# Five of 192 expert weight slabs loaded by two transfers of 8 partitions and one of 112

## The reference

```python
def ec_moe(u, w_router, w_gate, w_up, w_down):
    ...
    aff = jax.nn.softmax((u @ w_router).astype(jnp.float32), axis=-1)
    gates, idx = lax.top_k(jnp.swapaxes(aff, 1, 2), cap)
    xs = u[bidx, idx]
    hid = jax.nn.silu(jnp.einsum('becd,edf->becf', xs, w_gate)) * jnp.einsum('becd,edf->becf', xs, w_up)
    ys = jnp.einsum('becf,efd->becd', hid, w_down) * gates[..., None].astype(u.dtype)
    return jnp.zeros_like(u).at[bidx, idx].add(ys)
```

## Time and profile before

| what | value |
|---|---|
| median of three runs | 2798.47 us |
| profiled execution, its own time | 2803.4 us |
| its span in the trace | 2801.6 us |
| TensorE matmul busy | 2374.1 us, 85% |
| VectorE busy | 1193.8 us, 43% |
| mean rate of the transfers | 247 GB/s |

### The profile page before, as it was taken

One profiled execution on the slowest core, in us unless ns is written; L12 is line 12 of the kernel. 1 busy time (PEld: TensorE's weight loads), 2 busy tenths in 40 slices (PEclk: granted clock), 3 DMA queues, 4 the chain that ended last, 5 costly groups with the idle time before them and its releaser, 6 DMA issues.

```text
span 2801.6 us, 45258 instructions
## 1 busy us (share of the span) xinstructions
PE 2374.1 (85%) x19841; PEld 1843.7 (66%) x19841; DVE 1193.8 (43%) x2238; ACT 512.2 (18%) x1145; POOL 189.6 (7%) x322
## 2 busy tenths in 40 slices
PE   7999988555655665556899999999999999999999
PEld 4667774111211121111699988999999998899999
DVE  2555632000000000000566667774665666776555
ACT  4434421000000000000210125411011012451200
POOL 0363610000000000000000001000000000100000
PEclk9999989888887777877999999999999999999999
DMA  7534439999999999999644354344454444434443
GB/s 259 157 101 133 139 116 417 428 428 427 427 428 427 427 428 426 425 428 427 267 166 174 128 174 163 133 171 160 167 178 153 171 175 160 146 133 167 165 154 118
DMA packets 212625, 691.38 MB, mean 247 GB/s; under 512 B 36876, under 2 KB 76237, under 8 KB 186829
## 3 DMA queue, kind: packets, MB, share of 16 engines
q1 hardware_dynamic: 204685, 683.74, 63.3%
q10 hardware_dynamic: 7744, 4.75, 0.6%
HBM read 684.23 MB, written 4.23 MB: 246 GB/s over the span
## 4 chain that ended last, share of the span: by engine, by line
PE 62%; DMA 30%; DVE 4%; ACT 2%; issue 1%; SPq 0%; POOL 0%; ACTq 0%; DVEq 0%
PE bank L1958 18%; PE bank L2008 10%; DMA slab_ring_more<-in_moe_w_up 7%; PE bank L2210 6%; DMA slab_ring<-in_moe_w_up 6%; DMA slab_ring_more<-in_moe_w_gate 6%; PE bank L401 5%; DMA slab_ring_more<-in_moe_w_down 5%; DMA slab_ring<-in_moe_w_down 5%; PE bank L2303 4%; PE bank L1425 3%; PE bank L2051 3%; PE bank L1925 2%; PE bank L2106 1%; PE bank L2186 1%
## 5 line engine op out<-in xcount | busy, mean ns | idle before, releaser
L1425 PE MATMUL bank<-slab_ring,chosen_xT 128*32 128x512 f32 x1248 | 199.5, 775 | 123.3 <-DMA slab_ring<-in_moe_w_up 66.6
L1958 PE MATMUL bank<-slab_ring 128*128 128x128 f32 x2560 | 299.1, 275 | 1.8 <-ACT lru_gelu L2419 1.8
L1958 PEld LDWEIGHTS bank<-slab_ring 128*128 128x128 f32 x2560 | 292.3, 192 | 2.2 <-issue 2.2
L1587 DVE TENSOR_TENSOR beaten_then_hidden<-bank,beaten_then_hidden 128x512 f32<-128x512 f32 x16 | 11.1, 691 | 562.6 <-PE bank L1425 562.6
L1958 PE MATMUL bank<-layer_uT,slab_ring 128*128 128x128 f32 x1920 | 227.5, 275 | 0.0
L1958 PEld LDWEIGHTS bank<-layer_uT,slab_ring 128*128 128x128 f32 x1920 | 221.1, 192 | 0.2
L1425 PEld LDWEIGHTS bank<-slab_ring,chosen_xT 128*32 128x32 f32 x1248 | 38.9, 127 | 276.2 <-DMA slab_ring<-in_moe_w_up 110.7
L1425 PE MATMUL bank<-slab_ring_more,chosen_xT 128*32 128x512 f32 x800 | 135.4, 812 | 99.9 <-DMA slab_ring_more<-in_moe_w_up 56.8
L2008 PE MATMUL bank<-slab_ring 128*128 128x128 f32 x1408 | 165.7, 275 | 0.0
L2008 PEld LDWEIGHTS bank<-slab_ring 128*128 128x128 f32 x1408 | 161.4, 192 | 0.0
L1425 PEld LDWEIGHTS bank<-slab_ring_more,chosen_xT 128*32 128x32 f32 x800 | 25.2, 129 | 200.8 <-DMA slab_ring_more<-in_moe_w_up 87.3
(11 more groups left out here) (482 smaller groups left out, 3691.8 us busy)
## 6 DMA issues: line engine op xcount, KB each, us to landing
slab_ring<-in_w_up SPq DMA_DIRECT2D x44, 2048.0 KB, 8.0
slab_ring<-in_moe_w_up SPq DMA_DIRECT2D x39, 2048.0 KB, 46.2
slab_ring<-in_moe_w_gate SPq DMA_DIRECT2D x39, 2048.0 KB, 45.4
slab_ring<-in_moe_w_down SPq DMA_DIRECT2D x38, 2048.0 KB, 45.6
slab_ring<-in_w_in SPq DMA_DIRECT2D x28, 2048.0 KB, 7.9
slab_ring_more<-in_moe_w_down SPq DMA_DIRECT2D x26, 2048.0 KB, 46.8
slab_ring_more<-in_moe_w_gate SPq DMA_DIRECT2D x25, 2048.0 KB, 45.3
slab_ring_more<-in_moe_w_up SPq DMA_DIRECT2D x25, 2048.0 KB, 45.6
```

Source lines behind the costliest of these rows:

```text
L1425: ins = nc.tensor.matmul(out[32 * c:32 * c + 32, 0:cols], x, slot_of((q * EXPERT_SLABS + i) % NRE).rearrange("p (k n) -> p k n", k=2 if co ...
L1587: nc.vector.tensor_tensor(hid, ps[1][:, :], sg, ALU.mult).then_inc(ex.next("hidden"), 1)
L1958: i = nc.tensor.matmul(out[:, j * P:(j + 1) * P], a[:, k, j * P:(j + 1) * P], x[:, k, :], start=(start and j == 0 and k == 0), stop=(k == ...
```

## The change

Five slabs, the first gate slab of experts 3, 5, 7, 9 and 11 (n = 36, 60, 84, 108, 132), are each moved by three transfers in place of one: partitions 0 to 7, partitions 8 to 15, partitions 16 to 127. The same bytes go from the same place to the same place. The two small ones count on a semaphore of their own, the large one on the slot's. The tensor engine's program has one more wait ahead of each of the five slabs.

```diff
+NARROW_SLABS = tuple(e * EXPERT_SLABS for e in (3, 5, 7, 9, 11))
...
+    s_narrow = ctx.enter_context(nc.semaphore("narrow_slab_loaded"))
...
                 src = expert_slab(env, e, i)
-                sp.dma_start(slot_of(n % NRE).rearrange("p (k n) -> p k n", k=src.shape[1]), src).then_inc(env.full[n % NRE], 16)
+                to = slot_of(n % NRE).rearrange("p (k n) -> p k n", k=src.shape[1])
+                if n in NARROW_SLABS:
+                    for p in (0, 8):
+                        sp.dma_start(to[p:p + 8], src[p:p + 8]).then_inc(s_narrow, 16)
+                    sp.dma_start(to[16:], src[16:]).then_inc(env.full[n % NRE], 16)
+                else:
+                    sp.dma_start(to, src).then_inc(env.full[n % NRE], 16)
...
                 pe.wait_ge(env.full[n % NRE], 16 * ((n % NRE < EARLY_MOD) + n // NRE + 1))
+                if n in NARROW_SLABS:
+                    pe.wait_ge(s_narrow, 32 * (NARROW_SLABS.index(n) + 1))
```

## The result

The changed kernel takes **2845.22 us** (median of five, 2839.23 to 2855.4), the kernel before in the same comparison 2798.47 us. The ratio is 1.0163, with a 95% interval of 1.0152 to 1.0173: 46.75 us or 1.6% slower. The forecast was 2817, its range ended at 2828. The direction was right, the size was not: 18.5 us were forecast. The profiled execution of the changed kernel is its median one; that of the kernel before is 4.9 us above its median.

What follows compares the result with a forecast made beforehand. Expert stage bound by transfers until its last byte lands, TensorE afterwards. Five narrow slabs at 5.1 us add 25.5 us to leading engines, ending at 1373.0 against 1354.5: +18.5 us on 2798.5, 2817 us; range 2794 to 2828.

Steps and rivals of the forecast that it cites:

- TensorE as the judge of the landing: End of the expert stage: TensorE bounds what follows, so shifting the last slab's landing moves the kernel's end one to one.
- Ten more issues at nothing, the added wait at nothing: SP and TensorE in the expert stage: ten more issues and the added wait themselves cost nothing.
- Two halves of the engines, one ahead: Expert stage's end: about half the engines finish at 1346 to 1349 us, the others need until 1354.53.
- The side of the limit: Narrow writes in the expert stage: the limit lies on the side of SBUF, not in the engines.
- Partitions 0 to 15 are ... given ... to the leading eight: Narrow slabs: leading engines each carry 1 + 1 + 7 packets in place of 8, each of the others 7.
- The term of the 112: Transfer of 112 in each narrow slab: some packets meet, 0.9 us extra, between zero and 4.28.
- The term of the eights: Two eight-partition transfers per narrow slab: 2.4 us each on the leading engines, 0.61 us at full rate.
- The lagging engines gain 3 us which nobody sees: Expert stage: lagging engines carry fewer packets, gaining 3 us, hidden because the leading engines now finish last.
- No limit: Rival for the narrow writes: full rate, load simply balanced, -2.4 us, 2796 us; chance 0.26.
- A mild limit: Rival for the narrow writes: two engines meet, 1.22 us per transfer, +3.7 us, 2802; chance 0.10.
- A harder limit: Rival: 4.9 us per eight-partition transfer, +40.5 us, 2839; much the same with 2.4 us and the 112 at half rate; chance 0.08.
- The rival of a serializing pair: Rival: transfers spray over all sixteen engines and serialize; nothing shifts, +0 us, 2798.5; chance left inside 0.26.

Runs made afterwards that it cites:

- p8 kernels: Four variants of the kernel before: first slabs of experts 5 and 9 by sixteen eight-partition transfers, neighbours or 4 apart on written and read sides; 2820.7 to 2834.2 us.
- low_step: Kernel before, but first slabs of experts 5 and 9 load only partitions 0 to 63, by eight transfers of eight partitions 4 apart; 2799.6 us.
- low_next: Kernel before, but first slabs of experts 5 and 9 load only partitions 0 to 63, by eight transfers of eight neighbours; 2810.3 us.
- p8_ss: Kernel before, but first slabs of experts 5 and 9 by sixteen transfers of eight partitions, 4 apart on both written and read sides; 2828.0 us.
- s_16_112: Kernel before, but the five slabs each moved by one transfer of 16 and one of 112 partitions; 2842.6 us.
- only_112: Kernel before, but the five slabs load only partitions 16 to 127, by one transfer of 112; 2836.3 us.
- only_8_8: Kernel before, but the five slabs load only partitions 0 to 15, by two transfers of eight; 2791.3 us.
- s_64_64: Kernel before, but the five slabs each moved by two transfers of 64 partitions, 0 to 63 and 64 to 127; 2834.2 us.
- p8_dst_step: Kernel before, but first slabs of experts 5 and 9 by sixteen transfers of eight, written 4 apart and read as neighbours; 2820.7 us.
- p8_cc: Kernel before, but first slabs of experts 5 and 9 by sixteen transfers of eight, neighbours on both written and read sides; 2834.2 us.

## Why the prediction was wrong, point by point

- **TensorE as the judge of the landing: right.** "A shift of that landing moves the end of the kernel one to one": +45.2 us of landing, +41.8 us between the two profiled executions, whose remainders differ by 3.4 us.
- **Ten more issues at nothing, the added wait at nothing: right.** 3.62 us for the two, with SP waiting for TensorE both before and after.
- **Two halves of the engines, one ahead: right.** The landing marks of slab 191 in the kernel before are eight from 1346.4 to 1349.0 us and eight from 1352.9 to 1354.5.
- **The side of the limit: right for the eights.** It was read off stores and loads of 32 and 64 partitions as one of SBUF; the p8 kernels show it for large writes into partitions 0 to 63. The Trainium skill's "SBUF — State Buffer", section "Door 1: The DMA port swizzle (why `[64,N]` ≈ `[32,N]`)", gives the grouping of partitions that the step of 4 here was made from: four neighbours, and those 32 further, share a port. By that rule low_step has no meeting and low_next has; the runs agree, 426 against 240 GB/s. The 2.4 us that the forecast took for a transfer of eight, and also found by that rule, are not borne out: the packets of neighbouring eights took about 1.0 to 1.2 us.
- **"Partitions 0 to 15 are ... given ... to the leading eight": supported.** In p8_ss the last slab lands on one group of eight engines 17.0 us behind the other on the mean. The 32 packets more that one group carries are 19.6 us; less the lead of 6.2 us that it had that is 13.4, and if the lagging group had carried them it would be 25.8. But the leaders' load is a small part of the loss, as s_16_112 shows, and the step turned out not to matter.
- **The term of the 112 failed; it is the main miss.** It was taken at 0.9 us, between 0 and 4.28, by the argument "nearest is the transfer of 128". Measured (only_112): 7.7 us per slab on the mean of all engines, above the upper bound. That bound let the transfer's own seven packets take twice as long and left out that the engines are skewed: while one engine is in the transfer, all are slow, also in their shares of the slabs ahead and behind. The row that was nearest in form, the store from 64 partitions, had half of the rate, and should have been preferred to the transfer of 128, which is like it only in size.
- **The term of the eights was too large, and on the wrong engines.** 2 x 2.4 - 0.61 = 4.2 us on the leading eight was forecast. In only_8_8 a packet took about 1.2 us in place of 2.4, but on all sixteen engines, and 2.2 us per slab were lost on their mean.
- **"The lagging engines gain 3 us which nobody sees" failed, and with it the method.** The forecast kept an account for each half of the engines and took the later one. In the slow stretch all sixteen take 1.09 to 1.67 us per packet. In retrospect the sum that comes near is half of the slow stretch, a narrow slab at half rate (9.8 us) plus the skew. With the skew of 4 us read in the earlier trace rows it gives 6.9 us for the first slab, 6.7 measured. That is closer than it deserves: those rows are of expert 11, and at expert 3 the skew was 2.1 us, which gives 6.0.
- **Slips in the sums, without weight here.** The upper end, 2827, does not come from its parts: 1349 + 5 x (4.8 + 1.8 - 0.61) - 1354.5 is +24.5 us, 2823. And of the SP times called those of a small transfer, 1.8 us is a whole slab's; the small ones in the earlier trace rows took 2.9 and 6.1. The instruction fetches take 1.07 us each in the middle, 1.2 was worked out from a rounded share.
- **The rivals.** "No limit" is refuted. "A mild limit" had the time of a packet right, 1.22 us, and the total wrong, since it charged the leading engines alone and left the 112 out. "A harder limit", at 2839, had nearly the size, and its second form (the 112 at half rate) nearly the place; but it too charged the leading engines alone, so that its nearness is in part luck. It was given 0.08. The rival of a serializing pair, for which the Trainium skill's "DMA: Bandwidth & Descriptors", section "Rules for kernel authors", advises a single transfer of 128, gave +0 by the rows. The advice is borne out: two transfers of 64 lost 7.4 us per slab (s_64_64).
- **The view to look for** was "dips ... by some 5 us of half the engines"; seen were five stretches of 12 to 18 us with all engines at about half rate.

## What to carry to other kernels

In a stream that saturates the DMA engines, move whole tiles of 128 partitions. A transfer whose shares don't fall on the pattern of the 128 (here 112, 64, or eight neighbours) brings the rate of the whole core to about half until the slowest engine is through with it. For a slab split into 8 + 8 + 112, 16 + 112 or 64 + 64 this cost 6.7 to 10 us, where the slab streams in 4.9. Where split transfers can't be avoided, put them behind each other, so that the skew is paid once (25 us in place of 39). Partitions that are 4 apart and which no other engine is writing were free, shown here for 0 to 63 with the other half left out.
In a forecast, don't keep accounts per engine before a row shows that one engine can be slow without the others.

## What the runs showed that was not expected

- A meeting of writes in one group of partitions slows all sixteen engines alike, also those that write elsewhere: mostly 1.06 to 1.08 us per packet in low_next against 0.61. The Trainium skill's "DMA: Bandwidth & Descriptors", section "Back-pressure in remote DMA", says of another kind of transfer, between cores, that a saturated port holds up the engines that share its path. The runs here fit that in kind; where in the path all sixteen meet, none of them shows.
- The slow packets have several levels in place of 0.61 us: mostly 1.0 to 1.1 in eights of neighbours in partitions 0 to 63, about 1.25 in the second half of p8_ss and p8_dst_step, 1.50 to 1.63 in that of p8_cc (166 GB/s), and up to 1.93 in the first microseconds of s_16_112 (164 GB/s). A rule that gives all of them is not worked out.
- How the 112 partitions are dealt out to the engines was inferred (seven neighbours each), not seen; the records name no engine by its partitions.
- No version with all its bytes beats the kernel before. The lead of eight engines at the end of the stage remains unused: giving them the others' partitions is what, it seems, makes them meet.
